# A hybrid decoder block on one core: the path from the output projection to the experts ordered by token tile, with the opening and the end rearranged

## The reference, cut to what matters

```python
h = x + hybrid_mixer(rms_norm(x, g1), ...)        # proj = a @ w_in; GLA and dilated branches; @ w_mix_out
h = h + memory_cross_attention(rms_norm(h, g2), mem, ...)   # last step: o @ w_xo
f = rms_norm(h, g3)
# 256 tokens, 32 experts, top 4 of each token
logits = f @ w_router + b_router
top_logit, top_e = lax.top_k(logits, 4);  gate = softmax(top_logit)
y[e] = (min(f@w_gate[e]+b, 7) * sigmoid(1.702*...) * (clip(f@w_up[e]+b, -7, 7) + 1)) @ w_down[e] + b_down[e]
h = h + sum of gate * y over a token's four experts
out = rms_norm(h, g_final)
```

## Time and profile before

| | us |
|---|---|
| median of 3 runs | 1241.34 (1241.11 to 1243.54) |
| the profiled execution, its own time | 1242.41 |
| its span in the profile | 1240.7 |
| PE busy | 1153.2 (93%) |
| DVE busy | 411.6 (33%) |
| ACT busy | 261.6 (21%) |
| POOL busy | 20.9 (2%) |
| loads over the span | 458.38 MB, mean 369 GB/s |

### The profile page before, as it was taken

The page is one execution under the profiler, slowest core; times in us unless marked ns, Lnnn a source line. Parts: engine busy times, 40 slices in busy tenths (PEclk is TensorE's granted clock), DMA queues, the critical chain, the costliest instruction groups (busy, mean ns, idle before and its releaser), DMA issues.

```text
span 1240.7 us, 16139 instructions
## 1 busy us (share of the span) xinstructions
PE 1153.2 (93%) x6687; PEld 576.8 (46%) x6687; DVE 411.6 (33%) x803; ACT 261.6 (21%) x450; POOL 20.9 (2%) x40
## 2 busy tenths in 40 slices
PE   8999999999999999999989887998998898889887
PEld 7888989887433333333323232432332233224322
DVE  6789474665422222222122112211221122122112
ACT  5655464464400010010001000100110010001001
POOL 4000000000000000000000000000000000000000
PEclk9999999999899999999999999999999999999999
DMA  8455524986699999999999999999999999999996
GB/s 329 173 204 183 190 76 182 382 316 244 239 420 395 430 418 434 429 435 428 435 427 435 430 433 429 431 429 432 431 431 433 431 431 431 435 428 435 419 419 264
DMA packets 30117, 458.38 MB, mean 369 GB/s; under 512 B 3584, under 2 KB 3600, under 8 KB 8816
## 3 DMA queue, kind: packets, MB, share of 16 engines
q1 hardware_dynamic: 28800, 454.57, 87.8%
q0 software_dynamic: 832, 2.51, 0.6%
q10 hardware_dynamic: 432, 0.55, 0.1%
HBM read 456.57 MB, written 1.05 MB: 369 GB/s over the span
## 4 chain that ended last, share of the span: by engine, by line
PE 61%; DMA 29%; SPq 3%; issue 2%; ACT 2%; DVE 2%; POOL 0%; DVEq 0%; ACTq 0%; POOLq 0%
PE bank L1888 22%; DMA ring<-in_w_down 16%; DMA ring<-in_w_gate_up 12%; PE bank L1910 10%; PE bank L1495 4%; PE bank L1472 4%; PE sums L1553 3%; PE sums L1472 3%; SPq L431 3%; PE sums L1839 3%; PE sums L1495 2%; PE bank L1829 2%; PE bank L1553 2%; PE bank L1901 2%; DMA ring<-in_w_dense 1%
## 5 line engine op out<-in xcount | busy, mean ns | idle before, releaser
L1888 PE MATMUL bank<-ring,reg_a 128*64 128x512 f32 x2016 | 457.9, 606 | 42.5 <-DMA ring<-in_w_gate_up 41.8
L1888 PEld LDWEIGHTS bank<-ring,reg_a 128*64 128x64 f32 x2016 | 142.4, 139 | 324.4 <-issue 263.4
L1910 PE MATMUL bank<-ring,reg_ol 128*64 128x512 f32 x1024 | 227.0, 595 | 14.5 <-DMA ring<-in_w_down 12.8
L1389 DVE TENSOR_TENSOR masks<-bank,bT 128x256 f32<-128x256 f32 x64 | 27.2, 424 | 449.7 <-PE bank L1901 449.7
L1910 PEld LDWEIGHTS bank<-ring,reg_ol 128*64 128x64 f32 x1024 | 79.2, 137 | 141.1 <-issue 133.8
L625 ACT ACTIVATE reg_t<-bank 128x512 f32<-128x512 f32 x64 | 38.2, 597 | 440.5 <-PE bank L1888 240.5
L969 DVE SCALAR_TENSOR_TENSOR ring<-ring 128x2048 f16<-128x2048 f32 x47 | 107.3, 2289 | 40.1 <-ACT ring L643 39.8
L643 ACT ACTIVATE ring<-ring 128x2048 f16<-128x2048 f32 x47 | 89.5, 1910 | 32.7 <-PE sums L1553 14.1
L926 ACT ACTIVATE masks<-masks 128x256 f32<-128x256 f32 x64 | 26.7, 417 | 326.4 <-DVE masks L1390 326.4
L1839 PE MATMUL sums<-reg_t,reg_g 64*128 64x512 f32 x256 | 70.1, 634 | 5.5 <-ACT reg_t L625 5.5
L1376 DVE COPY reg_t<-bank 128x512 f32<-128x512 f32 x32 | 22.1, 691 | 159.2 <-PE bank L1888 159.2
(11 more groups left out here) (323 smaller groups left out, 884.8 us busy)
## 6 DMA issues: line engine op xcount, KB each, us to landing
ring<-in_w_gate_up SPq DMA_DIRECT2D x52, 4096.0 KB, 29.8
ring<-in_w_down SPq DMA_DIRECT2D x26, 4096.0 KB, 30.8
ring<-in_w_dense SPq DMA_DIRECT2D x47, 1024.0 KB, 5.1
ring<-in_w_gate_up SPq DMA_DIRECT2D x10, 2048.0 KB, 9.6
ring<-in_w_gate_up SPq DMA_DIRECT2D x16, 1024.0 KB, 25.5
ring<-in_w_down SPq DMA_DIRECT2D x6, 2048.0 KB, 11.0
ring<-in_w_gate_up SPq DMA_DIRECT2D x16, 512.0 KB, 14.2
ring<-in_w_down SPq DMA_DIRECT2D x12, 512.0 KB, 7.2
```

Source lines behind the costliest of these rows:

```text
L1888: ins = mm(pt[nh][col:col + 64, :], xg[:, c, j * SLOTS:(j + 1) * SLOTS], loaded(v + i, C, c), start=(c == 0), stop=(c == C - 1))
L1910: ins = mm(pt[2][64 * nh:64 * nh + 64, :], actT[:, 4 * i + c, :], w[:, nh * 512:(nh + 1) * 512], start=(i == 0 and c == 0), stop=(i == 1 a ...
```

## The change

Opening: the second tile of x is loaded from ACT's queue instead of SP's. q_g is written into two banks, the second half as a new fill `q_g1` in bank 7, and q_g and k_g run all chunks of high with high first, then high with low, then low with high. DVE makes all low parts of x before the second half of the first unit's low part.

From the output projection on: the fills go by token tile (xo00, xo10, xo01, xo11), g3 is multiplied into the router's weights by DVE, and PE waits for that before the first projection; transposes, router, choice, positions and selection are done for tile 0 while tile 1 is projected. Squares carry 1/D as a scale, so the mean takes one DVE step less. Four matmuls that write nothing of use (`awake`) stand around the positions.

End: the last expert's first two units come in four pieces instead of two, the scatter of the expert before goes ahead of its gates, three semaphores of early loads are reused for pieces, and the last norm's steps are reordered.

```diff
-FILLS = [f"x_T{i}" for i in range(4)] + ["q_g", "k_g", "alr", "v_g0", "v_g1", "r_g0", "r_g1", "lg"]
+FILLS = [f"x_T{i}" for i in range(4)] + ["q_g", "q_g1", "k_g", "alr", "v_g0", "v_g1", "r_g0", "r_g1", "lg"]
...
+ROUTING = {"fT0a": 2, "fT0b": 3, "rt0": 2, "fT1a": 0, "rl0": 3, "rt1": 2, "pos0": 3, "fT1c": 0, "fT1d": 1, "rl1": 2,
+           "pos1": 0, "all": 1}
...
+_TURNED = [f for f in FILLS if f != "q_g1"]
+BANK = {f: 4 + SUMS.index(f) if f in SUMS else ROUTING[f] if f in ROUTING else i % BANKS for i, f in enumerate(_TURNED)}
+BANK["q_g1"] = BANKS - 1
...
-        LAST_PIECES = {UPE * (EG - 1) + i: n for i, n in enumerate((2, 2, 4, 4, 2, 4))}
+        LAST_PIECES = {UPE * (EG - 1) + i: n for i, n in enumerate((4, 4, 4, 4, 2, 4))}
...
# SP, ACT
-            for t in range(TT):
-                sp.dma_start(h[:, t, :], xt_src[:, t, :]).then_inc(ld_x[t], 16)
+            sp.dma_start(h[:, 0, :], xt_src[:, 0, :]).then_inc(ld_x[0], 16)
+            act.dma_start(h[:, 1, :], A["x"][0, P:T, :]).then_inc(ld_x[1], 16)
...
# ACT, behind the Sin activations
                 if name == "q_g":
                     act.wait_ge(trig_in, 2)
-                unscaled(dst.rearrange("p a b -> p (a b)"), b[:]).then_inc(free_bank(name), 1)
+                    unscaled(dst[:, 0, :], b[:, 0:T]).then_inc(free_bank(name), 1)
+                    unscaled(dst[:, 1, :], take(act, "q_g1")[:, 0:T]).then_inc(free_bank("q_g1"), 1)
...
# ACT, from the projection to the experts
+            half_square(0, 0)
+            half_square(0, 1)
+            routed_T("0a")
+            token_highs(0)
+            half_square(1, 0)
+            router_part(0)
+            routed_T("1a")
+            half_square(1, 1)
+            router_part(1)
+            token_highs(1)
+            expert_exp(0)
+            expert_exp(1)
...
# DVE
-            for q in range(2):
+            for q in range(4):
                 low_T("x_T", q, aT, vT[:, 0:8])
             ahead_cut(AHEAD, HALF, w_high, 1, w_low)
-            for q in range(2, 4):
-                low_T("x_T", q, aT, vT[:, 0:8])
...
+            dve.tensor_tensor(w_rt[:], w_rt[:], bc(g3[:], E), ALU.mult).then_inc(consts, 1)
...
+            residual(0, 0)
+            residual(0, 1)
+            mean_square(0)
+            dve.memset(ranked[:, :, 0:TOPK], -FAR)
+            residual(1, 0)
+            routed_T("0b", 4, 4)
+            f_low_part(0, 0)
+            f_low_part(1, 0)
+            chosen(0)
+            residual(1, 1)
+            placed(0)
+            routed_T("1c", 4, 2)
+            mean_square(1)
+            routed_T("1d", 6, 2)
+            emptied(dve, "pos0")
+            selected(0, 0)
+            chosen(1)
             f_low_part(0, 1)
+            placed(1)
+            emptied(dve, "pos1")
...
+            dve.wait_ge(acc_full, 3)
+            gained(1, 0)
+            asked(0)
+            gained(0, 0)
+            asked(1)
...
# PE
+            highs_first([fill(name)[:, 0:T] for name in ("q_g", "q_g1")], cut_of("q_g"), (0, P), first_parts)
+            b = fill("k_g")
+            for i in range(2):
+                ins = highs_first([b[:, i * T:(i + 1) * T]], cut_of("k_g"), (i * P,), second_parts)
+            filled(ins, "k_g")
...
+            pe.wait_ge(consts, 8)
+            token_major("xo00", weights("xo0"), oxT, 4, (0,), 512, chunk_ready=pairs_ready("xpv"))
+            token_major("xo10", weights("xo1"), oxT, 4, (0,), 512)
+            token_major("xo01", weights("xo0"), oxT, 4, (1,), 512)
+            half_T("0a", range(4))
+            half_T("0b", range(4, C))
+            token_major("xo11", weights("xo1"), oxT, 4, (1,), 512, chunk_ready=second_tile)
+            router(1, range(4))
+            pe.wait_ge(gate_ready, 1)
+            filled(mm(fill("pos0")[:, 0:E], tri_s[:], mask[:, 0, :], start=True, stop=True), "pos0")
+            half_T("1c", range(4, 6))
+            half_T("1d", range(6, C))
...
+            awake(2)
+            pe.wait_ge(gate_ready, 2)
...
+            awake(2)
...
+                    if last and j == EG - 1:
+                        scatter(j - 1)
```

More of the change, by code:

```diff
@@ L1110, in _ @@
             emptied(dve, "q_g")
+            emptied(dve, "q_g1")
             emptied(dve, "k_g")
@@ new lines, in chosen, with placed @@
+                link(dve.memset(top[:, t, TOPK:], -FAR))
+                link(dve.match_replace(left[:, t, :], top[:, t, :], ranked[:, t, :], FAR))
+                dve.tensor_tensor(mask[:, t, :], logit[:, t, :], left[:, t, TOPK:], ALU.not_equal)\
+                    .then_inc(gate_ready, 1)
+            def placed(t):
+                b = take(dve, f"pos{t}")
+                dve.wait_ge(gate_ready, t + 1)
+                dve.scalar_tensor_tensor(place[:, t, :], b[:, 0:E], 1.0, mask[:, t, :], ALU.add, ALU.mult)\
+                    .then_inc(free_bank(f"pos{t}"), 1)
@@ L1349, in link2 @@
                     dve.wait_ge(z.moe_chain, k * LINKS + count[0])
-                for t in range(TT):
-                    ins = dve.tensor_tensor(sel[:, t, :].rearrange("p (e s) -> p e s", e=EG),
-                                            bc(place[:, t, bass.ds(n * EG, EG)], SLOTS), mid(iota_s[:], EG),
-                                            ALU.is_equal)
+                for t in (1,) if first else range(TT):
+                    ins = selected(t, n)
                 ins.then_inc(z.sel_ready, 1)
@@ L1513, in _, with highs_first, cut_of, first_parts @@
             norm_transposes("x_T", lambda t, c: xn[:, t, c * P:(c + 1) * P], ((norm_xn, 1), (norm_xn, 2)))
[L1515 to L1524 removed]
+            def highs_first(outs, w, cols, before):
+                for k, (pw, px) in enumerate(PASSES):
+                    for c in range(C):
+                        before(k, c)
+                        for b, o in zip(outs, cols):
+                            ins = mm(b, w[:, pw, c, o:o + P], aT[:, px, c, :], start=(k == 0 and c == 0),
+                                     stop=(k == 2 and c == C - 1))
+                            if k == 2 and c == C - 1 and len(outs) > 1:
+                                filled(ins, ("q_g", "q_g1")[o // P])
+                return ins
+            def cut_of(name):
+                return cut[HALVES.index(name) % EARLY].rearrange("p k (c n) -> p k c n", n=width(name))
+            def first_parts(k, c):
+                if k == 0:
+                    pe.wait_ge(x_high, c + 1)
+                    if c % (C // 2) == 0:
+                        pe.wait_ge(*((w_high, 1) if c else (ahead_act, 1)))
+                elif k == 1:
+                    pairs_ready("x_T")(c)
+                elif c % (C // 2) == 0:
+                    pe.wait_ge(*((w_low, 1) if c else (ahead_dve, 2)))
+            def second_parts(k, c):
+                if c == 0 and k == 0:
+                    pe.wait_ge(w_high, 2)
+                if c == 0 and k == 2:
+                    pe.wait_ge(w_low, 2)
+            highs_first([fill(name)[:, 0:T] for name in ("q_g", "q_g1")], cut_of("q_g"), (0, P), first_parts)
[3 more added lines that the diff above has]
+            filled(ins, "k_g")
             pe.wait_ge(consts, 7)
@@ new lines, in folded, with router @@
+            def folded(t, **flags):
+                emptied(pe, f"rt{t}")
+                return mm(pt[BANK[f"rl{t}"]][:, 0:E], rtp[:, t * P:(t + 1) * P], fold[:], **flags)
+            def router(t, chunks):
+                b = fill(f"rt{t}")
+                for c in chunks:
+                    if c % 4 == 0:
+                        emptied(pe, f"fT{t}{'ab'[c // 4]}")
+                    j = c % 4
+                    ins = mm(b[32 * j:32 * j + 32, 0:P], w_rt[:, c, :], fT[:, c, t * P:(t + 1) * P], start=(c < 4),
+                             stop=(c + 4 not in chunks))
+                filled(ins, f"rt{t}")
@@ L1858, in between @@
                         scatter_matrices(i)
-                    else:
+                    elif not (last and j == EG - 1):
                         scatter(j - 1, (i,))
```

221 lines of the change are left out of this document (92 added, 129 removed).

## The result

The changed kernel takes 1255.36 us (median of 4 runs, 1254.97 to 1256.85) beside 1241.6 us for the kernel before in the same comparison: a ratio of 1.011, 95% interval 1.0093 to 1.0128. It is slower by 13.8 us; the forecast was slower by 8.0, with 1253.3 us as the upper end of the range. The profiled execution took 1255.07 us, 12.66 more than the one of the kernel before.

A forecast was written before the change was run, and what follows sets the result against it. PE bounds the kernel until about 336 us, then the load stream, so PE's early loss reaches the end. Opening +9.3, handover -0.9, end -0.4 sum to +8.0 us: median 1249.3 us, range 1245.0 to 1253.3.

The forecast's parts named there:

- What bounds the kernel now: Whole kernel: PE bounds until about 336 us, then the load stream; PE's loss before the first expert reaches the end.
- The rival of absorption: Load stream: loads run ahead and absorb PE's pause, leaving only the end's -0.4 us; 1240.9 us, chance 0.03.
- Opening, the high passes: Opening: PE starts earlier on high parts, so the small product ends near 22.7 us, 2.4 us ahead.
- Opening, the second bank: Opening: PE waits at v_g0 until 33.9 us for ACT's copy of q_g1; 7.6 us remain after r_g1's wait goes.
- The price of the pause: v_g0's first matmuls: run at 1.2 instead of 2.4 GHz after PE's idle stretch; +1.7 us, bounds 0 and 1.9.
- Opening, sum: Opening: the bank wait's 7.6 us plus 1.7 us for the lower clock give +9.3 us, bounds 6.6 to 10.5.
- The handover: Output projection to the first group's second gather: four terms sum to about -0.9 us, or +1.9 if the clock falls.
- a, b and c: Up to the first gather: wait for router weights +1.8, extra PE work +1.45, shorter stretch after the fourth projection -1.5 us.
- d: First to second gather's end: clock staying at 2.4 GHz cuts the stretch from 8.5 to 5.8 us, -2.7.
- The fall: Handover rival: the clock falls there all the same, making the handover +1.9 us and the time 1252.1 us; chance 0.25.
- The first term, the product of the router's weights: Handover: first projection waits for DVE's gain in the router's weights, starting at 305.3 us; +1.8 us.
- The end: Behind the last load: ACT's first square starts about 0.4 us sooner, both tiles follow; -0.4 us, bounds 0 and -1.

The follow-up runs named there:

- e6: Changed kernel with ACT's copies of q_g and q_g1 ahead of the Sins and DVE's cut order of before; 1243.53 us, ratio 1.0015.
- e10: e9 plus two opening cuts moved out from behind waits (ACT's for r_g1, DVE's for r_g0); 1238.99 us, ratio 0.9986.
- e12: e2 (old opening) with the edits of e9 and e10; 1239.23 us, ratio 0.998.
- e4: Changed kernel with DVE's order of before (second half cut between second and third low part of x), bank wait kept; 1253.24 us, ratio 1.0093.
- e1: Kernel before with the change's new opening alone, handover and end as before; 1253.26 us, ratio 1.0096.
- e8: Changed kernel profiled once more, nothing altered; one execution, 1256.92 us.
- e5: Changed kernel with 56 matmuls of unused result filling PE's pause ahead of v_g0; 1253.8 us, ratio 1.0097.
- e2: Changed kernel with the old opening, handover and end still changed; 1242.33 us, ratio 1.0007.
- e9: e6 plus DVE's product of the router's weights moved to the start of cross attention; 1242.04 us, ratio 1.0002.
- e7: Kernel before profiled once more, nothing altered; one execution, 1244.55 us.
- e11: e10 without the four added `awake` matmuls; 1239.7 us, ratio 0.9987.

## Why the prediction was right or wrong

**What bounds the kernel now:** right. In all 14 profiles the stretch from the second gather to the last piece has one length within 3.5 us (898.3 to 901.8), while lg differs by 15 us: a late first expert reaches the end in full. The rival of absorption is out.

**Opening, the high passes:** right in kind; PE is through with the small product 1.7 us ahead, forecast 2.4 (96 matmuls took 11.17 us, not 10.8, and start 0.7 us earlier). With the pause gone this lead is worth nothing as long as the cuts hold r_g1 (e6), and 1.0 us in the profile once they are moved (e10 against e12).

**Opening, the second bank:** the wait, its place and what ends it were right, its length was not: it ended at 36.2 us, not at 33.9. This is the step that failed: "Nothing in this chain waits for PE, so a faster PE doesn't move it; it hangs on the load landed at 27.4 us. Its load might land 1 us earlier or later [...]; I take no shift." I had priced DVE's new order as one issue about 1 us late, with the fifth unit behind it (it was 1.7 us, and it is the fourth unit's). The chain has a second arm, the angle steps in front of the first Sin, and on DVE's queue these stand behind the cut of the fourth unit. Before, DVE had 3.67 us to spare there: the wait in front of L1046 in the earlier trace rows. The fourth unit was cut 25.28 - 19.25 = 6.03 us later, which used up the slack and 2.36 us more: 33.9 becomes 36.2. e4 puts the order back and gets 33.75.

**The price of the pause:** mis-sized, a second term that failed. Forecast 1.7 (0 to 1.9), measured 2.85 here, 1.6 to 2.9 over the four profiles with a pause (changed, e1, e4, e8); e5 shows that it is clock. The row that it was taken from the earlier trace rows was a group of 16 matmuls, too short to show how long the lower clock lasts: the bound of 1.9 was the bound of that row, not of the pause.

**Opening, sum:** forecast +9.3 (6.6 to 10.5), measured +12.66: v_g0 starts 36.23 - 25.10 = 11.13 us later, where 8.8 was forecast; its longer duration adds 2.85; the wait of 1.15 at r_g1 goes, as forecast, and 0.17 us of seams with it. These two terms, 2.3 us of pause and 1.15 of price, carry the opening past its upper bound.

**The handover:** forecast -0.9 with the clock up, +1.9 with it down (a, b and c are +1.7, d is -2.7); measured -1.1 in four profiles of the changed handover and +1.6 in three, 2.7 apart. With the clock up the terms were right one by one: in e6 the fourth projection ends at 317.87 us (forecast 318.2), the gather comes 6.5 us behind it (6.4), and the stretch to the second gather's end takes 5.8 (5.8). With the clock down the sum came out right by two errors that cancel: in e2 the gather comes 8.1 us behind the projection (forecast 6.4, for here the clock falls before the gather already), and the stretch takes 6.9 (forecast 8.5, for it is up again for the eight matmuls between the gathers, 1.94 us against 3.13). The fall had 0.25; it came in 3 of these 7, and in none of the four profiles with the product moved (e9 to e12). The first term, the product of the router's weights, was read rightly: e9 takes it out and gets 1.7 back. The Trainium skill (TensorE: Matmul & The Clock Gate, "Why this matters for your kernels") lays falls in mid-kernel to long idle gaps between bursts. The pause in the opening agrees with it (12.8 us, then 0.50). The handover of e2, e5 and e8 does not, where PE's gaps from the first projection on are 0.39 us at most, and neither does the group behind the bias product.

By an estimate, the handover's gain in the profiles is the clock's alone. In the old order the clock fell at the gather in all three profiles (before, e1, e7). An estimate from the earlier trace rows with the clock up, 1.66 us less for the gather and 1.19 less for the eight matmuls behind it (1.91 and 1.94 us in e6), puts the old order at about -2.9 us. That is 1.8 below the changed handover's -1.1, and level with the -2.8 of e9 to e12, where the product is moved. The new order kept the clock up in 8 of 11 profiles; why is not shown.

**The end:** forecast -0.4, measured -0.15 from the last piece to the end. The first square starts 0.8 us sooner behind the last piece (it waits 1.25 us against 2.07; forecast 0.4), but the second waits 0.56 for DVE and keeps only 0.15 of it: "both tiles follow" was wrong.

**The sum.** Profile against profile it was forecast at +8.0 and measured at +12.66: +3.4 in the opening, -0.2 at the handover, +1.25 in the tail (the clock behind the bias product, a fall for which the forecast had no term and which e7 shows in the kernel before as well), +0.2 at the end. The other 1.4 us of the miss in the median: the profiled execution of before lies 1.07 us above its median, that of the changed kernel 0.29 below.

**Versions that beat both:** e10 (0.9986), e11 (0.9987) and e12 (0.998), with the change's handover, its product moved, and two cuts of the opening moved. The gains are 0.13 to 0.2%. e12 shows that the change's opening isn't needed. Whether its handover is needed is untested: no run moves the two cuts in the kernel before and leaves the rest.

**Still open.** e6's opening and handover sum to -1.1 us, yet its median is 2 above that of before; e9's sum to -3.0, and its median is 0.8 above. The tail's clock explains 1.2 to 1.6 us of this if before mostly escapes that fall; e7 shows that it does not always. The clock over whole executions doesn't tell the two apart: the mean granted clock is 0.9861 in e6's ten runs and 0.9863 in the thirteen of before beside them. The profiles, one for each, don't settle the rest.

## What to carry to other kernels

An engine's step that is moved moves the loads that wait for it, and a load issued a little later can land much later, if another queue's large transfer gets in between: look at what every queue issues in that microsecond. Before a bank, slot or buffer gets a second user, read what stands ahead of its release in the releasing engine's program, and follow each arm of that chain, the ones with slack too. A product of constants that PE must wait for belongs well ahead of the last step before PE's start, not behind it. And a gain that one profile shows at a place where the clock can fall has to be compared with the other order at the same clock.

## What the runs showed of the hardware

The load of the fourth unit, 1 MB, was there 4.9 us after its issue at 14.11 us (e4); issued at 15.81, behind 1.4 MB of loads that POOL had issued since 14.32, it took 9.45 us. The clock fell at places where PE's gaps just before were far below a microsecond: at the new handover (1.03 or 1.59 us for the same four matmuls, gaps of 0.39 us at most) and behind eight matmuls of 32 rows with no gap (32 matmuls in 7.09 us in two profiles, 8.3 to 8.8 in the others that show all of them), in one execution of a kernel and not in another. After the pause of 12.8 us the granted clock stayed at 0.50 for another 6 us of unbroken matmuls in the changed kernel's profile; in e8, behind the same pause, it was up sooner (v_g0 in 7.03 us instead of 8.26).
